# Hybrid decoder layer on one core: latent attention by four heads, with the query and key weights stationary and the results written turned

## The chip, the core and the metric

The kernel runs on one core of one Trainium2 chip. The metric is the device time of one execution in microseconds (us); lower is better. All arithmetic is in float32. The large products are made from two halves of each operand in the format fp32r (a high part and the rest), as hi*hi + hi*lo + lo*hi.

## The reference, cut to what matters

```python
SEQ = 256; N_HEADS = 16; Q_LORA_RANK = KV_LORA_RANK = 512
QK_NOPE_DIM = 128; QK_ROPE_DIM = 64; V_HEAD_DIM = 128
...
q = (rmsnorm(q_lat, g_q_a) @ w_q_b).reshape(B, S, N_HEADS, QK_NOPE_DIM + QK_ROPE_DIM)
q_nope, q_pe = q[..., :QK_NOPE_DIM], q[..., QK_NOPE_DIM:]
kv = (rmsnorm(c_kv, g_kv_a) @ w_kv_b).reshape(B, S, N_HEADS, QK_NOPE_DIM + V_HEAD_DIM)
k_nope, v = kv[..., :QK_NOPE_DIM], kv[..., QK_NOPE_DIM:]
...
q_pe = apply_rope(q_pe, cos, sin); k_pe = apply_rope(k_pe, cos, sin)
s = (einsum('bhqd,bhkd->bhqk', qn, kn) + einsum('bhqr,bkr->bhqk', qp, k_pe)) * scale
s = where(key_idx[None, :] <= q_idx[:, None], s, -inf)
o = einsum('bhqk,bhkd->bhqd', softmax(s), vh)
...
y_a = o @ w_attn_br
merged = sigmoid(gate_a) * y_a + sigmoid(gate_p) * y_p
```

`q_lat`, `c_kv`, `gate_a` and `gate_p` are columns of `rmsnorm(x) @ w_in`. The rest of the layer (pooling branch, memory cross-attention, feed-forward part) is the same in both kernels.

## The kernel before

All weights stream from memory in units. A unit is 2 contraction tiles of 128 rows times up to 512 columns. Two units make a chunk, which SyncE loads into one of four slots of `raw` (L403). For each unit ScalarE writes the high half `whi` (L1126, called hi below), VectorE the low half `wlo` (L1608, called lo), and TensorE multiplies (L571). There are four slots of `whi` and `wlo`: at step k ScalarE and VectorE prepare unit k + 4, and hi(k + 4) waits until TensorE is through with unit k (semaphore `w_used`). All orders are written out by hand; each engine waits on counting semaphores.

The attention loop has 4 turns (L728 on TensorE, L1264 on ScalarE, L1746 on VectorE, L449 on SyncE) of 2 pairs of heads. A pair has 12 units: units 0 and 1 make the queries of two heads (2 x 192 = 384 columns), units 2 and 3 keys and values of two heads (512 columns), units 4 to 11 a column of 512 of a gate. In all of them the activations (`lat` or `actA`, 128 tokens) are stationary and the weights move: for each contraction tile and each half t of the 256 tokens three matmuls (L566 to L568). The results land token by token in the two banks `acc`; half t = 0 of a unit is done before half t = 1, and ScalarE copies each half out (`evac`, L1140), which frees it for TensorE (`acc_out[t]`). Since the scores need queries and keys with the feature on the partitions, TensorE turns them:

```python
if k in (5, 6):            # head h = k - 5
    ...
    for t in range(TT):
        pe.transpose(at[(fs + h) % 2][:, t * P:(t + 1) * P],
                     q_sb[:, t, h * (NOPE + ROPE):h * (NOPE + ROPE) + NOPE], ident[:, :])
        mm = pe.transpose(at[(fs + h) % 2][:, S + t * P:S + (t + 1) * P],
                          kv_sb[:, t, 2 * h * P:(2 * h + 1) * P], ident[:, :])
```

After unit 6 two more transposes turn the rotated columns `qpe`, which VectorE made (`rotate`, L1662). Scores stand after units 7 and 8 (L764, L765), the transposes of the probabilities after unit 10 (L772), and the product with the values after unit 11 (L781, L783), that is behind the last unit of the gate. The gate of the first pair goes through a sigmoid into `bufX`, that of the second into `gp_sb`; GpSimd then multiplies `bufY` with `gp_sb` (L534). After the loop TensorE goes on with `w_attn_br` (`V_YA`), in the same two banks `acc`.

Ahead of the loop, ScalarE copies the latents to `zlat` and squares them, and TensorE turns the raw `zlat` into `lat`; the norm of each token (`rstd` of `N_Q` and `N_C`, L1635) is applied only at the copy out of queries, keys and values. The feed-forward input, further on, already has the other form that the change brings here: the weights stationary, both halves of the activations moving (512 columns, L979), and a second matmul of 256 columns with the low weights (L981). ScalarE copies one half of its result out (L1507), VectorE adds the other (L1978).

Of the kernel before, what the change touches and what calls it, by code (L numbers as in the profile page):

```python
# [35 lines left out]
AHEAD = 4  # L36
WARM_UP = 12
# [6 lines left out]
def hybrid_layer(nc, a, out, x3_spill):  # L44
# [15 lines left out]
    QPAIR = 2 * (NOPE + ROPE)  # L60
# [11 lines left out]
    V_YA = V_ATT + NH // 2 * 12  # L72
# [32 lines left out]
    U_YA = U_ATT + 3 * NH // 2  # L105
# [17 lines left out]
    A_MK = A_PAIR + 5 * NH // 2  # L123
# [13 lines left out]
    w_in, w_qb, w_kvb = rows("w_in"), rows("w_q_b"), rows("w_kv_b")  # L137
# [12 lines left out]
    def sem(name):  # L150
# [52 lines left out]
    q_sb = sb(pairs, "q_sb", [P, TT, QPAIR])  # L203
    kv_sb = sb(pairs, "kv_sb", [P, TT, NC])
    qkT = sb(pairs, "qkT", [P, 2, 2 * S])
    qpeT = sb(pairs, "qpeT", [P, S])
    qpe = sb(pairs, "qpe", [P, TT, 2 * ROPE])
# [55 lines left out]
    rdiag = cu[:, 1, :].rearrange("p (t s) -> p t s", t=TT)  # L263
    mq_sb = kch[:, :, :]
# [27 lines left out]
        "rope_step", "trig_ok", "abs_ok", "rope_ok", "ang_ok"))  # L292
    s_filled, s_max, s_nmax, s_exp, s_rsum, s_norm = (sem(n) for n in (
# [108 lines left out]
    def _(sp):  # L402
        def load(c, cs, src, n, kts=4):  # L403
# [4 lines left out]
            if n == NC:  # L408
                dst = raw[:, s, :, :].rearrange("p u (k n) -> p (u k) n", n=n)[:, 0:kts, :]
                sp.dma_start(dst, src).then_inc(w_loaded[s], 32)  # L410
            else:
                per = kts // 2
                for h in range(2):
                    dst = raw[:, s, h, 0:per * n].rearrange("p (k n) -> p k n", n=n)
                    sp.dma_start(dst, src[:, h * per:(h + 1) * per, :]).then_inc(w_loaded[s], 16)
# [33 lines left out]
        with sp.Fori(0, NH // 4) as i:  # L449
            for m in range(2):  # L450
                c = V_ATT // 2 + 12 * i + 6 * m
                load(c, 6 * m, w_qb[:, :, bass.ds(i * 2 * QPAIR + m * QPAIR, QPAIR)], QPAIR)
                load(c + 1, 6 * m + 1, w_kvb[:, :, bass.ds(i * 2 * NC + m * NC, NC)], NC)
                for j in range(4):
                    load(c + 2 + j, 6 * m + 2 + j,
                         w_in[:, 4 * j:4 * j + 4, bass.ds(i * NC + (C_GA, C_GP)[m], NC)], NC)
# [37 lines left out]
    def _(pool):  # L494
# [39 lines left out]
        with pool.Fori(0, ND) as i:  # L534
            for t in range(TT):
                pool.wait_ge(acc_out[t], U_ATT + 6 * i + 6)
# [19 lines left out]
    def _(pe):  # L556
# [71 lines left out]
        for v in range(16):  # L628
# [11 lines left out]
            if v in (10, 12):  # L640
                pe.wait_ge(acc_out[0], U_LAT + 1)
                pe.wait_ge(acc_out[1], U_LAT + 1)
# [85 lines left out]
        with pe.Fori(0, NH // 4) as i:  # L728
            for m in range(2):
                v, u, f = V_ATT + 24 * i + 12 * m, U_ATT + 6 * i + 3 * m, A_PAIR + 10 * i + 5 * m  # L730
                pair, fs = 2 * i + m, A_PAIR + 5 * m
                for k in range(12):
                    if k < 2:
                        unit(v + k, k, lambda h, kt: lat[:, h, kt, :], (2 * k, 2 * k + 1), QPAIR, u, k == 0, k == 1)
                    elif k < 4:
                        unit(v + k, k, lambda h, kt: lat[:, h, KL + kt, :], (2 * k - 4, 2 * k - 3), NC, u + 1,
                             k == 2, k == 3)
                    else:
                        unit(v + k, k, lhsA, (2 * k - 8, 2 * k - 7), NC, u + 2, k == 4, k == 11)
                    if k in (5, 6):  # L740
                        h = k - 5
                        for t in range(TT):
                            pe.wait_ge(acc_out[t], u + 2)
                        at_wait(f + h)
                        if k == 6:
                            pe.wait_ge(rope_ok, pair + 2)
                            at_wait(f + 2)
# [1476 lines left out]
```

## Time and profile before

| | us |
|---|---|
| median of 3 runs | 1797.07 (1796.44 to 1797.71) |
| the profiled execution: its own time | 1795.94 |
| its span in the trace | 1794.2 |
| TensorE busy | 1780.8 (99% of the span) |
| VectorE busy | 1155.4 (64%) |
| ScalarE busy | 951.6 (53%) |
| TensorE's granted clock | 0.999 of full |

The attention loop stands from about 164.8 to 469 us of the span. Matmuls overlap in the trace: what one costs is the distance between the starts of neighbours, not its duration. Where the next block has another shape, the cost of a short group is the start of the second matmul behind it, less where that would have stood without the group.

### The profile page before, as it was taken

The numbers are of one execution on the slowest core, as the hardware profiler recorded it, in microseconds if no ns is written. First come the engines' busy times: TensorE is split into PE (matmuls) and PEld (weight loads), VectorE is DVE, ScalarE is ACT, GpSimd is POOL, SyncE is SP. The second block draws the span as 40 slices with busy tenths as digits, with TensorE's granted clock in tenths as the row PEclk, the third lists the DMA queues.
The fourth block names the chain that finished last, engine by engine and source line by source line (L and its number), as shares of the span: only waits on it lengthen the run. The fifth ranks groups of instructions, "written<-read, shape, count | busy, mean of one in ns | idle before, by whom it ended". The sixth has DMA issues, their size and how long they took to land.

```text
span 1794.2 us, 25047 instructions
## 1 busy us (share of the span) xinstructions
PE 1780.8 (99%) x8758; PEld 1491.4 (83%) x8758; DVE 1155.4 (64%) x1608; ACT 951.6 (53%) x1295; POOL 59.4 (3%) x128
## 2 busy tenths in 40 slices
PE   9999999999999999999999999999999999999998
PEld 7888888888888888888888878888888888888786
DVE  5554555555465554454555477777777777788887
ACT  7555556665545655544555474444444444455554
POOL 4000000000000110000000100000000000000002
PEclk9999999999999999999999999999999999999999
DMA  8455544455466555555444546555555555656565
GB/s 287 153 188 176 166 162 148 156 170 168 167 222 221 201 189 176 183 173 190 154 146 158 189 166 232 187 187 187 187 187 187 187 187 187 199 167 206 190 197 189
DMA packets 167021, 330.74 MB, mean 184 GB/s; under 512 B 8454, under 2 KB 14006, under 8 KB 165558
## 3 DMA queue, kind: packets, MB, share of 16 engines
q1 hardware_dynamic: 165414, 318.48, 53.3%
q10 hardware_dynamic: 1552, 11.54, 1.6%
q8 instruction: 33, 0.54, 0.1%
q14 instruction: 22, 0.18, 0.0%
HBM read 325.81 MB, written 4.19 MB: 184 GB/s over the span
## 4 chain that ended last, share of the span: by engine, by line
PE 97%; DVE 1%; ACT 1%; DMA 0%; issue 0%; DVEq 0%; ACTq 0%
PE bank L566 17%; PE bank L979 17%; PE bank L568 17%; PE bank L567 17%; PE bank L981 9%; PE bank L1027 4%; PE bank L1028 4%; PE bank L1029 4%; PE bank L598 1%; PE bank L764 1%; PE bank L765 1%; PE bank L781 0%; PE bank L772 0%; DVE wlo L1605 0%; DVE actA L1926 0%; DMA bufX<-in_x 0%
## 5 line engine op out<-in xcount | busy, mean ns | idle before, releaser
L1605 DVE TENSOR_TENSOR wlo<-raw,whi 128x1024 fp32r<-128x1024 f32 x520 | 641.7, 1236 | 556.0 <-ACT whi L1138 433.0
L1138 ACT ACTIVATE whi<-raw 128x1024 fp32r<-128x1024 f32 x400 | 424.0, 1060 | 502.7 <-PE bank L568 293.0
L979 PE MATMUL bank<-actA,whi 128*128 128x512 f32 x1344 | 472.0, 394 | 0.0
L981 PE MATMUL bank<-actA,wlo 128*128 128x256 f32 x1344 | 380.1, 283 | 0.0
L979 PEld LDWEIGHTS bank<-actA,whi 128*128 128x128 f32 x1344 | 252.4, 188 | 58.3
L566 PE MATMUL bank<-whi,actA 128*128 128x512 f32 x672 | 273.2, 406 | 1.6 <-DVE wlo L1605 0.6
L568 PE MATMUL bank<-whi,actA 128*128 128x512 f32 x672 | 265.3, 395 | 0.0
L567 PE MATMUL bank<-wlo,actA 128*128 128x512 f32 x672 | 265.0, 394 | 0.0
L981 PEld LDWEIGHTS bank<-actA,wlo 128*128 128x128 f32 x1344 | 252.7, 188 | 0.0
L566 PE MATMUL bank<-whi,actB 128*128 128x512 f32 x576 | 229.2, 398 | 0.3 <-DVE actB L1620 0.3
L568 PE MATMUL bank<-whi,actB 128*128 128x512 f32 x576 | 227.3, 395 | 0.0
L567 PE MATMUL bank<-wlo,actB 128*128 128x512 f32 x576 | 227.2, 395 | 0.0
L1124 ACT ACTIVATE whi<-raw 128x1024 fp32r<-128x1024 f32 (+1 forms) x120 | 125.0, 1047 | 105.0 <-PE bank L568 90.7
L1543 ACT ACTIVATE whi<-raw 128x1024 fp32r<-128x1024 f32 x105 | 111.2, 1062 | 101.7 <-PE bank L1029 84.0
L566 PEld LDWEIGHTS bank<-whi,actA 128*128 128x128 f32 x672 | 126.6, 188 | 30.6 <-DVE wlo L1605 2.0
L568 PEld LDWEIGHTS bank<-whi,actA 128*128 128x128 f32 x672 | 126.4, 188 | 29.7
L2053 DVE TENSOR_TENSOR wlo<-raw,whi 128x1024 fp32r<-128x1024 f32 x105 | 129.2, 1232 | 31.5 <-ACT whi L1543 31.0
L567 PEld LDWEIGHTS bank<-wlo,actA 128*128 128x128 f32 x672 | 126.8, 189 | 26.6
L568 PEld LDWEIGHTS bank<-whi,actB 128*128 128x128 f32 x576 | 108.5, 188 | 25.5
L566 PEld LDWEIGHTS bank<-whi,actB 128*128 128x128 f32 x576 | 108.5, 188 | 24.6 <-DVE actB L1620 0.5
L567 PEld LDWEIGHTS bank<-wlo,actB 128*128 128x128 f32 x576 | 108.6, 188 | 24.3
L1027 PE MATMUL bank<-whi,gT 128*128 128x512 f32 x282 | 111.3, 395 | 0.4 <-DVE y L2131 0.4
(278 smaller groups left out, 1869.5 us busy)
## 6 DMA issues: line engine op xcount, KB each, us to landing
raw<-in_w_ffn_in SPq DMA_DIRECT2D x88, 1024.0 KB
raw<-in_w_in SPq DMA_DIRECT2D x48, 1024.0 KB
raw<-in_w_ffn_out SPq DMA_DIRECT2D x84, 512.0 KB, 4.9
raw<-in_w_mem_kv SPq DMA_DIRECT2D x32, 1024.0 KB
raw<-in_w_attn_br SPq DMA_DIRECT2D x16, 1024.0 KB
raw<-in_w_mix_out SPq DMA_DIRECT2D x16, 1024.0 KB
raw<-in_w_mem_q SPq DMA_DIRECT2D x16, 1024.0 KB
raw<-in_w_mem_o SPq DMA_DIRECT2D x16, 1024.0 KB
```

The source lines that it names most:

```text
L566: pe.matmul(acc[t][:, 0:n], hi, wh, start=f, stop=False)
L567: pe.matmul(acc[t][:, 0:n], hi, wl, start=False, stop=False)
L568: mm = pe.matmul(acc[t][:, 0:n], lo, wh, start=False, stop=l)
L979: pe.matmul(dst[:, :], whi[:, s, o:o + P], actA[:, :, kt, :], start=(kt == 0), stop=False)
L981: mm = pe.matmul(dst[:, 0:S], wlo[:, s, o:o + P], actA[:, 0, kt, :], start=False, stop=(kt == KD - 1))
L1027: pe.matmul(dst, hi, wh, start=first, stop=False)
L1028: pe.matmul(dst, hi, wl, start=False, stop=False)
L1124: act.activation(whi[:, vs % AHEAD, 0:w], raw[:, c, vs % 2, 0:w], ACT.Copy).then_inc(hi_done, 1)
L1138: act.activation(whi[:, ks % AHEAD, 0:w], raw[:, c, ks % 2, 0:w], ACT.Copy).then_inc(hi_done, 1)
L1543: act.activation(whi[:, n % AHEAD, :], form_at(u), ACT.Copy).then_inc(hi_done, 1)
L1605: dve.tensor_tensor(wlo[:, vs % AHEAD, 0:w], raw[:, c, vs % 2, 0:w], f32(whi[:, vs % AHEAD, 0:w]), ALU.subtract).then_inc(lo_done, 1)
L2053: dve.tensor_tensor(wlo[:, n % AHEAD, :], form_at(FOUT[n]), f32(whi[:, n % AHEAD, :]), ALU.subtract).then_inc(lo_done, 1)
```

## The change

The loop keeps 4 turns of 24 units, now for four heads at once: units 0 and 1 queries without the rotated columns, 2 and 3 rotated columns of four heads (256 columns), 4 and 5 keys, 6 and 7 values, 8 to 15 the gate of the pooled branch (`gp_sb`), 16 to 23 the gate of the attention branch (`bufX`). For queries and keys (`heads_unit`) the weights are stationary and the latents move, so that the results come out turned, in four banks, 2 to 5. Queries and keys use the same four banks one after the other. ScalarE copies the first 256 columns of each bank out (`heads_out`) and VectorE adds the others, behind its lo of the same step. The 16 transposes of a turn for queries and keys go. The two pairs of a turn (`pair_job`) then run behind units 6 to 12 and 14 to 20. Since keys and queries are turned, a token's norm can't be applied at the copy out any more: VectorE scales `zlat` itself (`latent_norm`), and TensorE's transposes of `zlat` wait for it (`z_ok`). A chunk of queries, rotated columns, keys or values is loaded by four DMAs with runs of 128 or 64 floats (`head_load`).

```diff
-    w_in, w_qb, w_kvb = rows("w_in"), rows("w_q_b"), rows("w_kv_b")
+    w_qb = a["w_q_b"][0].rearrange("(k p) (h n) -> p k h n", p=P, n=NOPE + ROPE)
+    w_kvb = a["w_kv_b"][0].rearrange("(k p) (h n) -> p k h n", p=P, n=NOPE + VD)
...
+        def head_load(c, cs, src, n):
+            s = cs % RAW_SLOTS
+            sp.wait_ge(lo_done, 2 * c - 2 * RAW_SLOTS + 2)
+            for k in range(4):
+                dst = raw[:, s, k // 2, k % 2 * QUAD * n:(k % 2 + 1) * QUAD * n].rearrange("p (h n) -> p h n", n=n)
+                sp.dma_start(dst, src[:, k, :, :]).then_inc(w_loaded[s], CHUNK_IN // 4)
...
@@ TensorE
             if v in (2, 4):
-                pe.wait_ge(acc_out[0], U_LAT + 2)
-                pe.wait_ge(acc_out[1], U_LAT + 2)
+                pe.wait_ge(z_ok, 4)
                 t_fill(T_C + (v - 2) // 2, (v - 2) // 2, zlat[:, 1, :, :], v - 2)
...
+        def heads_unit(v, vs, part_, k, first_filled):
+            s = vs % AHEAD
+            pe.wait_ge(lo_done, v + 1)
+            for b in range(2):
+                for kk in range(2):
+                    for j in range(2):
+                        o = kk * NC + (2 * b + j) * P
+                        kt = part_ + 2 * k + kk
+                        to = bank[2 + 2 * b + j]
+                        pe.matmul(to[:, :], whi[:, s, o:o + P], lat[:, :, kt, :], start=(k == 0 and kk == 0), stop=False)
+                        mm = pe.matmul(to[:, 0:S], wlo[:, s, o:o + P], lat[:, 0, kt, :],
+                                       start=False, stop=(k == 1 and kk == 1))
+                if b == 0 and k == 1:
+                    mm.then_inc(first_filled, 1)
+            mm.then_inc(w_used, 1)
...
+        with pe.Fori(0, NQ) as i:
+            v, u = V_ATT + 24 * i, U_ATT + 4 * i
+            for k in range(24):
+                if k < 2:
+                    if k == 0:
+                        pe.wait_ge(t_out, T_O + 2 * i)
+                    heads_unit(v + k, k, 0, k, q_filled)
+                elif k < 4:
+                    unit(v + k, k, lambda h, kt: lat[:, h, kt, :], (2 * k - 4, 2 * k - 3), QROPE, u, k == 2, k == 3)
+                elif k < 6:
+                    if k == 4:
+                        pe.wait_ge(q_sum, 2 * i + 2)
+                    heads_unit(v + k, k, KL, k - 4, k_filled)
+                elif k < 8:
+                    unit(v + k, k, lambda h, kt: lat[:, h, KL + kt, :], (2 * k - 12, 2 * k - 11), NC, u + 1,
+                         k == 6, k == 7)
+                else:
+                    c = k % 8
+                    unit(v + k, k, lhsA, (2 * c, 2 * c + 1), NC, u + 1 + k // 8, c == 0, c == 7)
+                for m in range(2):
+                    pair_job(i, m, k - 8 - 8 * m)
...
@@ ScalarE
+                if k == 1:
+                    heads_out(q_filled, i + 1, v + 2, [qT[:, 2 * b:2 * b + 2, :] for b in range(2)], q_copied_out)
...
+                if k == 15:
+                    act.wait_ge(k_sum, 2 * i + 2)
+                    evac(u + 2, v + 15, [gp_sb[:, t, :] for t in range(TT)], N_X, func=ACT.Sigmoid)
+                if k == 23:
+                    evac(u + 3, v + 23, [bufX[:, t, bass.ds(i * NC, NC)] for t in range(TT)], N_X, func=ACT.Sigmoid)
+                hi_at(V_ATT, i, 24, k)
...
@@ VectorE
+        def latent_norm(n, j):
+            dve.wait_ge(rstd_done, normed(n))
+            for t in range(TT):
+                dve.tensor_scalar(zlat[:, j, t, :], zlat[:, j, t, :], rstd[:, n, t:t + 1], None,
+                                  ALU.mult).then_inc(z_ok, 1)
...
+            for k in range(24):
+                lo_at(V_ATT, i, 24, k)
+                if k == 1:
+                    for b in range(2):
+                        dve.wait_ge(q_copied_out, 2 * i + b + 1)
+                        q = qT[:, 2 * b:2 * b + 2, :]
+                        dve.tensor_tensor(q, q, psum[:, 2 + 2 * b:4 + 2 * b, S:2 * S], ALU.add).then_inc(q_sum, 1)
```

**Between the queries and what uses the banks next.** On TensorE, after the change, these rows stand where the rotated columns (moving weights, 256 columns) end and the first key unit begins (stationary `whi`, moving `lat`).

```order
L588 MATMUL bank<-whi,lat 128x256
L586 MATMUL bank<-whi,lat 128x256
L587 MATMUL bank<-wlo,lat 128x256
L588 MATMUL bank<-whi,lat 128x256
L814 REGISTER_ALU
L749 REGISTER_ALU [waits q_sum]
L756 MATMUL bank<-lat,whi 128x512 [waits lo_done]
L757 MATMUL bank<-lat,wlo 128x256
```

The first key unit waits for `q_sum`, which VectorE gives after these rows, the first of a turn (lo of units 4 and 5, then the two additions). Before, the place of the additions was empty and no unit of the loop waited for VectorE to add.

```order
L1657 TENSOR_TENSOR wlo<-raw,whi 128x1024 [waits hi_done]
L1652 REGISTER_ALU
L1657 TENSOR_TENSOR wlo<-raw,whi 128x1024 [waits hi_done]
L1847 ISA
L1849 TENSOR_TENSOR qT<-qT,bank 128x512 [waits q_copied_out]
L1847 REGISTER_ALU
L1849 TENSOR_TENSOR qT<-qT,bank 128x512 [waits q_copied_out]
```

**Between the two gates.** On TensorE, before the change, the last unit of a pair's gate is followed by the product with the values, and then by the next unit in the banks `acc`:

```order
L568 MATMUL bank<-whi,actA 128x512
L776 REGISTER_ALU
L587 REGISTER_ALU [waits at_out]
L781 MATMUL bank<-probT,kv_sb 128x256 [waits t_out]
L783 MATMUL bank<-probT,kv_sb 128x128
L781 MATMUL bank<-probT,kv_sb 128x256
L783 MATMUL bank<-probT,kv_sb 128x128
L573 REGISTER_ALU
L561 REGISTER_ALU [waits lo_done]
L566 MATMUL bank<-whi,lat 128x384 [waits acc0_out]
L567 MATMUL bank<-wlo,lat 128x384
```

After it, the last unit of the first gate (unit 15) is followed at once by the first of the second gate (unit 16), which waits for bank 0 of `acc`:

```order
L586 MATMUL bank<-whi,actA 128x512
L587 MATMUL bank<-wlo,actA 128x512
L588 MATMUL bank<-whi,actA 128x512
L593 REGISTER_ALU
L581 REGISTER_ALU [waits lo_done]
L586 MATMUL bank<-whi,actA 128x512 [waits acc0_out]
L587 MATMUL bank<-wlo,actA 128x512
```

What moved: the four matmuls with `probT` stand behind units 12 and 20 now, and nothing stands between units 15 and 16. The same holds between unit 23 of the last turn and the first unit of `w_attn_br`.

**The copy out of a gate on ScalarE.** Before, the first pair's gate goes to `bufX`; the wait is an instruction of its own ahead of the load of the function table. After, the first gate of a turn goes to `gp_sb`, and the wait stands on the activation, behind the load (in the kernel before, the second pair's gate, to `gp_sb`, stands so too).

```order
L1185 ACTIVATE probT<-bank 128x384 [waits at_filled]
L1146 REGISTER_ALU [waits rstd_done]
L1150 ISA [waits acc0_ready]
L1150 ACT_TABLE_LOAD
L1150 ACTIVATE bufX<-bank,rstd 128x512
```

```order
L1176 ACTIVATE whi<-raw 128x1024 [waits w_used]
L1222 REGISTER_ALU
L1223 ACTIVATE qpeT<-bank 128x256 [waits at_filled]
L1342 REGISTER_ALU
L1184 REGISTER_ALU [waits rstd_done,k_sum]
L1188 ACT_TABLE_LOAD
L1188 ACTIVATE gp_sb<-bank,rstd 128x512 [waits acc0_ready]
```

## Rows read from the trace of the kernel before

**Rows 1.** The page, part 4: the chain that ended last.

```profile
PE 97%; DVE 1%; ACT 1%; DMA 0%; issue 0%; DVEq 0%; ACTq 0%
```

**Rows 2.** Waits of TensorE's weight loads, 170 to 440 us.

```profile
PEld bank L772 <- DVE prob L1768: 1.3, 7, 0.2
```

**Rows 3.** Timeline of TensorE: four transposes after a unit.

```profile
256.79 0.27 PE L749 MATMUL bank<-ident,q_sb 128*128 128x128 f32 x1
...
257.46 0.39 PE L567 MATMUL bank<-wlo,actA 128*128 128x512 f32 x1
```

**Rows 4.** Timeline of TensorE: 23 matmuls of 384 columns between these starts.

```profile
241.59 0.34 PE L567 MATMUL bank<-wlo,lat 128*128 128x384 f32 x1
...
245.63 0.39 PE L566 MATMUL bank<-whi,lat 128*128 128x512 f32 x1
```

**Rows 5.** Timeline of TensorE: 24 matmuls of 256 columns between these starts.

```profile
899.00 0.28 PE L885 MATMUL bank<-kvh,mqr 128*128 128x256 f32 x1
...
901.87 0.39 PE L566 MATMUL bank<-whi,actA 128*128 128x512 f32 x1
```

**Rows 6.** Timeline of TensorE: 17 pairs of 512 and 256 columns between.

```profile
1199.85 0.39 PE L979 MATMUL bank<-actA,whi 128*128 128x512 f32 x1
...
1205.81 0.40 PE L979 MATMUL bank<-actA,whi 128*128 128x512 f32 x1
```

**Rows 7.** Timeline of TensorE: the second half of a gate's last unit.

```profile
276.67 0.40 PE L566 MATMUL bank<-whi,actA 128*128 128x512 f32 x1
...
278.06 0.60 PE L781 MATMUL bank<-probT,kv_sb 128*128 128x256 f32 x2
```

**Rows 8.** Timeline of ScalarE: queries copied out, last unit done.

```profile
245.83 0.58 ACT L1150 ACTIVATE q_sb<-bank,rstd 128x384 f32<-128x384 f32 x1 [0.40 <-PE bank L568]
```

**Rows 9.** Timeline of ScalarE in the feed-forward part.

```profile
1212.77 1.09 ACT L1507 ACTIVATE asum<-bank 128x512 f32<-128x512 f32 x2 [1.31 <-PE bank L981]
1213.74 1.06 ACT L1138 ACTIVATE whi<-raw 128x1024 fp32r<-128x1024 f32 x1
```

**Rows 10.** Timeline of VectorE in the feed-forward part.

```profile
1214.83 1.22 DVE L1605 TENSOR_TENSOR wlo<-raw,whi 128x1024 fp32r<-128x1024 f32 x1 [2.43 <-ACT whi L1138]
1215.97 0.68 DVE L1998 TENSOR_TENSOR gT<-cu,gT 128x512 f32 x1
1216.58 1.23 DVE L1605 TENSOR_TENSOR wlo<-raw,whi 128x1024 fp32r<-128x1024 f32 x1
```

**Rows 11.** Timeline of ScalarE: first copy out of the loop.

```profile
169.02 1.03 ACT L1150 ACTIVATE q_sb<-bank,rstd 128x384 f32<-128x384 f32 x2
```

**Rows 12.** Timeline of TensorE: it waits for that copy.

```profile
168.91 0.34 PE L568 MATMUL bank<-whi,lat 128*128 128x384 f32 x1
169.63 0.51 PE L566 MATMUL bank<-whi,lat 128*128 128x512 f32 x1 [0.38 <-ACT q_sb L1150]
169.98 0.39 PE L567 MATMUL bank<-wlo,lat 128*128 128x512 f32 x1
```

**Rows 13.** Timeline of ScalarE: the two gates, and a copy of 256 columns.

```profile
238.53 1.28 ACT L1150 ACT_TABLE_LOAD   x1
239.82 1.26 ACT L1150 ACTIVATE gp_sb<-bank,rstd 128x512 f32<-128x512 f32 x2
...
276.96 1.28 ACT L1150 ACT_TABLE_LOAD   x1 [0.50 <-PE bank L568]
...
299.62 0.38 ACT L1185 ACTIVATE qpeT<-bank 128x256 f32<-128x256 f32 x1
```

**Rows 14.** Groups of VectorE by line and form: busy us, mean ns, idle before.

```profile
L1768 DVE TENSOR_SCALAR prob<-prob,rsum 128x256 f32<-128x256 f32 x16 | 5.6, 348 | 0.0
```

**Rows 15.** Timeline of VectorE: the norm of the key latents.

```profile
66.77 0.17 DVE L1635 RECIPROCAL rstd<-std 128x2 f32<-128x2 f32 x1 [0.27 <-ACT std L1161]
```

**Rows 16.** Timeline of TensorE: the transposes of the key latents.

```profile
67.45 0.60 PE L598 MATMUL bank<-ident,zlat 128*128 128x128 f32 x4
```

**Rows 17.** Stretch of 2 us: engines, clock, DMA share, GB/s (columns of 64).

```profile
80.00:82.00 2.00, 2.00 (x10) 1.64 (x9) 1.14 (x1) 1.52 (x2) 0.00 (x0) 1.00 0.58 131
```

More of the change, by code:

```diff
@@ L59, in hybrid_layer @@
     NF = DFF // NC
[L60 removed]
+    QUAD = 4
+    NQ = NH // QUAD
+    QROPE = QUAD * ROPE
     SCALE = float((NOPE + ROPE) ** -0.5)
@@ L202, in hybrid_layer @@
     pairs = ExitStack()
-    q_sb = sb(pairs, "q_sb", [P, TT, QPAIR])
-    kv_sb = sb(pairs, "kv_sb", [P, TT, NC])
-    qkT = sb(pairs, "qkT", [P, 2, 2 * S])
+    qr_sb = sb(pairs, "qr_sb", [P, TT, QROPE])
+    v_sb = sb(pairs, "v_sb", [P, TT, NC])
+    qT = sb(pairs, "qT", [P, QUAD, S])
     qpeT = sb(pairs, "qpeT", [P, S])
-    qpe = sb(pairs, "qpe", [P, TT, 2 * ROPE])
+    qpe = sb(pairs, "qpe", [P, 2, TT, 2 * ROPE])
     prob = sb(pairs, "prob", [P, 2, 3 * P])
@@ L263, in hybrid_layer @@
     rdiag = cu[:, 1, :].rearrange("p (t s) -> p t s", t=TT)
+    k_half = [gp_sb[:, b, :].rearrange("p (h s) -> p h s", h=2) for b in range(TT)]
     mq_sb = kch[:, :, :]
@@ new lines, in normalise, with pair_job @@
+        def normalise(n, h):
+            dve.wait_ge(s_exp, 2 * n + 2)
+            dve.reciprocal(rsum[:, h, :], ssum[:, h, :]).then_inc(s_rsum, 1)
+            dve.wait_ge(s_rsum, n + 1)
+            for t in range(TT):
+                o = slice(t * P, (2 * t + 1) * P)
+                dve.tensor_scalar(prob[:, h, o], prob[:, h, o], rsum[:, h, t:t + 1], None,
+                                  ALU.mult).then_inc(s_norm, 1)
+        def pair_job(i, m, k):
+            pair = 2 * i + m
+            if k == 0:
+                row_max(2 * pair, 0)
+            if k == 1:
+                row_max(2 * pair + 1, 1)
+                normalise(2 * pair, 0)
+            if k == 2:
+                normalise(2 * pair + 1, 1)
+            if k == 4:
+                t_split(T_O + pair, T_O + m, *tiles(actB, 4 * i + 2 * m))
@@ new lines, in _ @@
+        with dve.Fori(0, NQ) as i:
+            for k in range(24):
+                lo_at(V_ATT, i, 24, k)
+                if k == 1:
+                    for b in range(2):
+                        dve.wait_ge(q_copied_out, 2 * i + b + 1)
+                        q = qT[:, 2 * b:2 * b + 2, :]
+                        dve.tensor_tensor(q, q, psum[:, 2 + 2 * b:4 + 2 * b, S:2 * S], ALU.add).then_inc(q_sum, 1)
+                if k == 5:
+                    for b in range(2):
+                        dve.wait_ge(k_copied_out, 2 * i + b + 1)
+                        dve.tensor_tensor(bufX[:, b, bass.ds(i * NC, NC)].rearrange("p (h s) -> p h s", h=2), k_half[b],
+                                          psum[:, 2 + 2 * b:4 + 2 * b, S:2 * S], ALU.add).then_inc(k_sum, 1)
+                if k in (3, 4):
+                    m, pair = k - 3, 2 * i + k - 3
+                    if m == 0:
+                        for t in range(TT):
+                            dve.wait_ge(acc_out[t], U_ATT + 4 * i + 1)
+                    rotate([qr_sb[:, :, (2 * m + h) * ROPE:(2 * m + h + 1) * ROPE] for h in range(2)],
+                           [qpe[:, m, :, h * ROPE:(h + 1) * ROPE] for h in range(2)], steps[0] + pair, pair + 1)
+                for m in range(2):
+                    pair_job(i, m, k - 8 - 8 * m)
```

249 lines of the change are left out of this document (105 added, 144 removed).

## The prediction

> **What bounds the kernel now.** I read the page first, and there the chain that ended last: 97% of it is TensorE [rows 1]. The reader is to see that a microsecond of TensorE work saved or a microsecond of waiting added on TensorE moves the end, and that nothing else does. Then the waits of TensorE's weight loads over the attention loop: in 270 us the only entry is the wait for the normalised probabilities, 7 times, 1.3 us in all [rows 2]. So ScalarE and VectorE stay ahead of TensorE throughout the loop, with little to spare where a chain of theirs is long. Last I read the timelines of the three engines, row by row, over one turn of the loop and over the feed-forward part, which already has the form that is brought in here.
>
> **What TensorE no longer does, and what it does in another form.** Four transposes start at 256.79; the second matmul behind them starts at 257.46, where it would have stood at 256.79 + 0.23 = 257.02. So four cost 0.44 us, 0.11 each [rows 3]. 16 a turn, 64 in all go: **-7.0 us**. The multiplications keep their columns (43008 a turn) but are cut otherwise. Prices from starts: 384 columns (245.63 - 241.59)/23 = 0.1757 us [rows 4]; 512 columns (278.06 - 276.67)/6 = 0.232 [rows 7]; 256 columns (901.87 - 899.00)/24 = 0.1196 [rows 5]; a pair of 512 and 256 with stationary weights (1205.81 - 1199.85)/17 = 0.3506 [rows 6]. A turn before: 48 x 0.1757 + 48 x 0.232 = 19.57. After: 32 x 0.3506 + 24 x 0.1196 + 24 x 0.232 = 19.66. Four turns: **+0.3 us**. The row for 256 columns is of stationary activations and moving fp32r, as the rotated columns are; were they bound by the weight load instead, a turn's 24 would take more, but the wait of the next paragraph would shrink by the same amount.
>
> **The wait for the query sums.** Keys go into the banks in which the queries still lie, and between the two stand only the two short units of rotated columns, 24 x 0.1196 = 2.87 us. Count from S, the start of the first of these units. ScalarE sees unit 1 done 0.20 later (245.83 against 245.63) [rows 4, 8]. It copies the second half of the queries out and then makes hi of unit 5: in the feed-forward part the second of two such copies takes (1213.74 - 1212.77)/2 = 0.49, so hi starts at S + 0.69 [rows 9]. VectorE's lo starts 1.09 behind hi (1214.83 against 1213.74), at S + 1.78; the next operation starts 1.14 later, at S + 2.92; one of 512 columns takes 0.68 and its neighbour starts after 0.61 [rows 9, 10]. So the two additions end at S + 2.92 + 0.61 + 0.68 = S + 4.21. From a release to where TensorE effectively goes on it takes 0.15: the first copy of the loop starts at 169.02 and its first half is out 0.58 later, at 169.60, and the matmul after the next starts at 169.98, that is 0.23 behind an effective start of 169.75 [rows 8, 11, 12]. The key unit starts at S + 4.36 instead of S + 2.87: 1.5 us a turn, **+6.0 us**. Queued behind it are all of TensorE's later units; what is late next on ScalarE (hi of unit 8, which waits for unit 4) has four units of lead, and its lo comes 6 us ahead of need. The key sums lie in the open: between them and their first reader stand units 6 to 8.
>
> **The wait between the two gates.** Before, the product with the values stood behind each gate's last unit, and the copy out with its sigmoid lay under it; no wait for it is in the trace [rows 2]. After, unit 16 follows unit 15 and needs bank 0. Count from U, where unit 15's predecessor ends and the two transposes of `qpe` start: unit 16 would start at U + 0.22 + 2.78 = U + 3.00. ScalarE starts hi of unit 18 at U + 0.20, is free for the copy of `qpe` about 1.0 later and through with it at U + 1.6 [rows 13]. The load of the table then isn't held by unit 15 (238.53 follows the copies without a gap) and the sigmoid starts 1.29 behind it; two copies out take 1.26, the first some 0.67 [rows 13]. Bank 0 is free at U + 1.6 + 1.29 + 0.67 = U + 3.55, TensorE goes on at U + 3.70: 0.7 a turn, **+2.7 us**.
>
> **At the loop's end** the first unit of `w_attn_br` follows unit 23 directly. That gate goes to `bufX`, and there the load is held by the first half: it starts 0.29 after the second half's first matmul (276.96 against 276.67) [rows 7, 13]. Bank 0 is free 0.29 + 1.29 + 0.67 = 2.25 after that point, TensorE goes on at 2.40 instead of 1.39: **+1.0 us**, once. Between turns there is no such wait, since unit 0 writes to other banks and unit 2 comes 5.6 us later.
>
> **At the loop's start** the queries before waited for their own predecessor's copy: 169.75 against a start of 168.91 + 0.18 = 169.09. The two query units now use no bank that ScalarE still has to read: **-0.7 us** [rows 12].
>
> **The norm of the latents.** The reciprocal starts at 66.77 and takes 0.17; two scalings of 512 columns follow. The nearest row is such a scaling of 256 columns, 0.35 [rows 14, 15]. Below: two of that row overlap, and there is next to no wait. Above: at the rate of an operation with two tensors, 66.97 + 0.61 + 0.68 = 68.26, TensorE's transposes going on at 68.41 instead of 67.45 [rows 10, 16]: 1.0 us. I take 0.47 for one and 0.38 to the next, done at 67.8: **+0.5 us**. The query latents have more room, two whole units, and cost nothing; the cover there is the two units between their squares and their transposes, and without it they would cost the whole chain, some 2 us.
>
> **At nothing:** the copies out of queries and keys (ScalarE has four copies fewer of turned tiles), the other place of the pairs (scores, exponentials and transposes keep their distances in units, so the waits of [rows 2] stay), GpSimd's product in mid-turn (it lies beside lo of unit 19, which has two units of lead), and the loads.
>
> **The sum:** -7.0 + 0.3 + 6.0 + 2.7 + 1.0 - 0.7 + 0.5 = +2.8, with the digits kept +2.9. On the profiled execution's 1795.94 (its span is 1794.2) that is 1798.8; the median of the runs shown is 1.1 higher, so I predict 1797.07 + 2.9 = **1800.0 us**. 0.2%, which is about what a measurement can tell here, is 3.6 us: faster is below 1793.5, slower above 1800.7.
>
> **The loads and a rule against them.** A 2 us stretch with two loads in runs of 256 bytes shows 131 GB/s at a busy share of 0.58, so 226 GB/s at full share [rows 17]. A chunk of 1 MB at that rate takes 4.6 us, and each has about six units, some 16 us, from its issue to its use. Cost nothing; bounds: nothing, and the rival below.
>
> The Trainium skill ("DMA: Bandwidth & Descriptors", Specifications) wants at least 512 bytes for line rate, and below that has a read-modify-write; the rotated columns come in 256 bytes. By the rule that chunk is slow in a way that it gives no figure for; the row above bears out a lower rate, and the rival takes it up.
>
> **Rivals.**
> *Slower, by the table load (0.20).* If unit 15 holds the load of the table, as with `bufX` [rows 13], each turn's wait is 2.25 + 0.15 - 1.39 = 1.0 instead of 0.7. For it: an exponential's table stands in between in both cases, and the row that speaks against it has other copies ahead. Price 4 x 0.33 = 1.3: 1801.3, slower. It decides from 0.2 us a turn on.
> *Slower, by a longer change of table (0.02).* Five copies out on TensorE's path carry a load. If a change took twice the 1.29 of [rows 13], each would end 1.29 later: +6.5, 1806.5. Against it: in both rows the sigmoid, or what ScalarE does next, starts when the load is over.
> The Trainium skill ("ScalarE: Activation LUTs", What ACT_TABLE_LOAD costs) has such a rule: it adds a drain of 1380 ns to the 1283 ns of the load, which would make the sum, as an estimate, 1807. The trace agrees with the 1283, and shows no drain: 1.29 from the load's start to the sigmoid's.
> *Slower, by late loads (0.06).* Four chunks a turn come in four pieces each, 16 issues of SyncE in a row. If their data came at a third of the rate above, a 1 MB chunk would take 14 us, four 56, and the eight units that use them last 20, with 16 of lead: some 20 us a turn. At half the rate they take 37, and the wait is about 1 us a turn: 1804. Against it: the share of 0.58 for small runs.
> *Faster (0.07).* The sums are ready in time: if VectorE's additions came ahead of TensorE, the 6.0 would go: 1794.0, and with half of the gate's wait gone too 1792.6. Against it: the additions stand behind lo of unit 5 in the order, and lo can't start before hi. It needs three of the steps in my chain to be shorter by a third.
> *Half of the wait (0.10).* The chain from S is shorter by 0.7 us, because the copy or lo starts sooner: 1797.1, no change.
> *The forecast (0.55)*, own range 1798.4 to 1801.6 by 0.3 either way in each of five waits; a quarter of it is above 1800.7.
>
> **The numbers.** Faster 0.07. Slower 0.20 + 0.02 + 0.06 + a quarter of 0.55 = 0.42. Same: three quarters of 0.55 + 0.10 = 0.51. The range 1796 to 1803 holds the forecast, the half wait and the held load, 0.85, and leaves out the others.
>
> **What would show it.** After: no transposes of queries and keys; the weight loads of the first key matmul wait for VectorE's addition 4 times, some 1.5 us each; those of the second gate's first unit wait for the copy to `gp_sb` 4 times, 0.7 each, and of `w_attn_br` once for `bufX`, 1.0; one wait of 0.5 for `zlat`; the query wait at 169 gone; rotated columns at 0.12 a matmul; no wait of hi for a load. I am wrong if another wait appears in the loop, if the key wait is under 1 us, or if hi waits for data.

## The result, and the profile after

| | before | after |
|---|---|---|
| median | 1796.82 us (20 runs, 1795.89 to 1797.71) | 1799.61 us (20 runs, 1798.71 to 1800.32) |
| span of the profiled execution | 1794.2 us | 1797.6 us |

The ratio is 1.0015, with a 95% interval of 1.0009 to 1.0021: the changed kernel is 2.8 us slower. Forecast were +2.9 and 1800.0 us. By the border that the prediction sets itself (slower above 1800.7) this counts as no change; the interval nevertheless excludes 1.

The page of the changed kernel, its first lines and part 4 (the chain that ended last):

```profile
span 1797.6 us, 25146 instructions
PE 1776.7 (99%) x8758; PEld 1483.8 (83%) x8758; DVE 1165.5 (65%) x1628; ACT 941.2 (52%) x1279; POOL 60.7 (3%) x128
PE 95%; DVE 2%; ACT 1%; issue 1%; DMA 0%; DVEq 0%; ACTq 0%
```

TensorE is busy for 4 us less than before and the span is longer: it has less to do and waits more. The chain of [rows 1] has fallen from 97% to 95% TensorE; 1% more is VectorE's, and 1% is "issue" (TensorE or another engine waiting for nothing that the profile shows).

The waits of TensorE's matmuls over the whole of the changed kernel (us in total, times, longest) say for what:

```profile
PE bank L756 <- DVE qT L1849: 5.3, 4, 1.3
PE bank L586 <- ACT gp_sb L1188: 1.7, 4, 0.4
...
PE bank L586 <- ACT bufX L1188: 0.8, 1, 0.8
...
PE bank L618 <- DVE zlat L1693: 0.3, 1, 0.3
```

None of these four was there before, and each is one that the prediction names. The waits of the weight loads in the attention loop, against [rows 2]:

```profile
PEld bank L756 <- issue: 6.1, 4, 1.5
PEld bank L586 <- ACT gp_sb L1188: 3.4, 4, 0.9
PEld bank L788 <- DVE prob L1826: 1.5, 8, 0.2
PEld bank L586 <- issue: 1.2, 1, 1.2
```

The wait for the probabilities is as it was (1.5 us in 8 waits, 1.3 in 7 before). The wait for the copy at the start of the loop [rows 12] has gone.

**The key unit's wait.** Timeline of turn 2 (start, duration, engine, line); rows of TensorE between the first and the last of the rotated columns' matmuls are left out:

```profile
247.27 0.28 PE L586 MATMUL bank<-whi,lat 128*128 128x256 f32 x1
...
247.47 0.60 ACT L1309 ACTIVATE qT<-bank 128x512 f32<-128x512 f32 x1 [0.57 <-PE bank L757]
...
247.96 2.00 ACT L1176 ACTIVATE whi<-raw 128x1024 fp32r<-128x1024 f32 x2
...
249.04 1.23 DVE L1657 TENSOR_TENSOR wlo<-raw,whi 128x1024 fp32r<-128x1024 f32 x1 [1.36 <-ACT whi L1176]
...
250.00 0.28 PE L588 MATMUL bank<-whi,lat 128*128 128x256 f32 x1
...
250.19 1.28 DVE L1849 TENSOR_TENSOR qT<-qT,bank 128x512 f32<-128x512 f32 x2
...
251.60 0.49 PE L756 MATMUL bank<-lat,whi 128*128 128x512 f32 x1 [1.31 <-DVE qT L1849]
...
251.93 0.27 PE L757 MATMUL bank<-lat,wlo 128*128 128x256 f32 x1
```

Read it down: copy of the queries, hi of unit 5 (at S + 0.69, S being 247.27), lo of unit 5, the two additions, and only then keys. TensorE was through with the rotated columns at 247.27 + 24 x 0.119 = 250.13 and goes on effectively at 251.93 - 0.23 = 251.70: 1.57 us, forecast 1.5. The other three turns show the same 1.57.

**The wait between the gates.** ScalarE in turn 1, then TensorE:

```profile
212.47 1.28 ACT L1188 ACT_TABLE_LOAD   x1
213.77 1.27 ACT L1188 ACTIVATE gp_sb<-bank,rstd 128x512 f32<-128x512 f32 x2
```
```profile
213.69 0.39 PE L588 MATMUL bank<-whi,actA 128*128 128x512 f32 x1
214.51 0.51 PE L586 MATMUL bank<-whi,actA 128*128 128x512 f32 x1 [0.42 <-ACT gp_sb L1188]
214.85 0.39 PE L587 MATMUL bank<-wlo,actA 128*128 128x512 f32 x1
```

The table load is not held by the gate's last unit; the sigmoid starts 1.30 behind it. The matmul after the next stands at 214.85, where an unbroken stream has it at 213.69 + 2 x 0.232 = 214.15: 0.7 us, and 0.67 to 0.70 in the other turns. At the loop's end the load is held by the unit, as forecast, and the same reckoning gives 472.29 - (470.74 + 0.46) = 1.09 us (ScalarE, then TensorE):

```profile
469.85 1.28 ACT L1188 ACT_TABLE_LOAD   x1 [0.41 <-PE bank L588]
```
```profile
470.74 0.40 PE L588 MATMUL bank<-whi,actA 128*128 128x512 f32 x1
471.98 0.47 PE L586 MATMUL bank<-whi,actB 128*128 128x512 f32 x1 [0.84 <-ACT bufX L1188]
472.29 0.39 PE L587 MATMUL bank<-wlo,actB 128*128 128x512 f32 x1
```

The key latents' transposes are late too: the second matmul behind them starts at 68.64 instead of 68.12, 0.5 us. The Trainium skill ("ScalarE: Activation LUTs", What ACT_TABLE_LOAD costs) has 1283 ns for the load, and the trace agrees (1.28 us). The drain of 1380 ns that the same section adds is in no row here: the sigmoid starts 1.30 us behind the start of the load.

### The profile page after: what moved, and what is told of

It is laid out like the page before. It is cut to its first block, busy times and chain, and to the rows that moved or that the text cites. A ratio compares the mean times of both kernels' runs of the same rounds, so it can differ in the third digit from the quotient of the medians.

```text
span 1797.6 us, 25146 instructions
## 1 busy us (share of the span) xinstructions
PE 1776.7 (99%) x8758; PEld 1483.8 (83%) x8758; DVE 1165.5 (65%) x1628; ACT 941.2 (52%) x1279; POOL 60.7 (3%) x128
## 2 busy tenths in 40 slices
DMA packets 192237, 330.75 MB, mean 184 GB/s; under 512 B 17286, under 2 KB 43318, under 8 KB 190774
## 4 chain that ended last, share of the span: by engine, by line
PE 95%; DVE 2%; ACT 1%; issue 1%; DMA 0%; DVEq 0%; ACTq 0%
PE bank L1017 17%; PE bank L586 16%; PE bank L588 16%; PE bank L587 16%; PE bank L1019 9%; PE bank L1065 4%; PE bank L1066 4%; PE bank L1067 4%; PE bank L756 2%; PE bank L618 1%; PE bank L757 1%; PE bank L779 1%; PE bank L781 1%; PE bank L797 0%; PE bank L788 0%
```

## The experiments

The third column is the kernel before on the same chip. "Span" is that of the profiled execution. The runs stand on several chips, on which the kernel before took between 1796.11 and 1796.90 us, so a difference of medians between two rows can be off by some tenths; the spans are given beside it where it matters.

| run | median | before | span |
|---|---|---|---|
| additions first | 1793.31 | 1796.90 | 1791.6 |
| gates split | 1793.32 | 1796.90 | 1792.0 |
| both | 1787.21 | 1796.90 | 1785.8 |
| before, 48 transposes less | 1791.13 | 1796.90 | 1788.7 |
| additions later | 1808.39 | 1796.11 | 1807.0 |
| plain loads | 1799.47 | 1796.11 | 1797.2 |
| both, key latents later | 1786.61 | 1796.11 | 1784.9 |
| 32 bytes | 1796.78 | 1796.45 | 1795.0 |
| both, no tile | 1789.56 | 1796.45 | 1787.7 |
| 64 bytes | 1788.21 | 1796.45 | 1786.4 |
| 32 bytes ahead of the weights, 32 behind | 1796.84 | 1796.45 | 1795.0 |
| all, 64 bytes | 1777.86 | 1796.75 | 1775.3 |

### The wait for the query sums

```diff
-                lo_at(V_ATT, i, 24, k)
                 if k == 1:
                     for b in range(2):
                         dve.wait_ge(q_copied_out, 2 * i + b + 1)
                         ...
                         dve.tensor_tensor(q, q, psum[...], ALU.add).then_inc(q_sum, 1)
+                lo_at(V_ATT, i, 24, k)
```

> The changed kernel with VectorE's two additions of the query sums put ahead of the subtraction of unit 5, and nothing else moved. In the changed kernel the key transposes of every turn wait for these sums: the second addition ends when the clock row of the trace has it at 251.5 in turn 2, and TensorE stands still for 251.93 - 0.23 - 250.13 = 1.57 us there, 6.28 us over four turns. My theory: with the additions first they end one subtraction (1.2 us and its wait for the rounded weights) sooner, the wait goes, and the kernel takes about 6.2 us less than the changed one, some 3.4 us less than the kernel before: 1793.4 us. Rival one: the wait is set by the sums of TensorE or by ScalarE's copy and not by the order on VectorE; then nothing changes (1799.6). Rival two: the subtraction that now comes later holds unit 5's low weights back by about as much as was won; then the wait moves to the first product of unit 5 and the time is between 1797 and 1799.6.

Measured 1793.31, ratio to before 0.9978 (0.9969 to 0.9987), so 6.3 us under the changed kernel, where 6.2 were expected. VectorE in turn 2 of this kernel:

```profile
246.04 1.28 DVE L1848 TENSOR_TENSOR qT<-qT,bank 128x512 f32<-128x512 f32 x2
247.49 2.36 DVE L1657 TENSOR_TENSOR wlo<-raw,whi 128x1024 fp32r<-128x1024 f32 x2 [0.17 <-ACT whi L1176]
```

The additions fill the time in which VectorE waited for hi, the subtraction behind them is on time, and no wait for `qT` is left. The term of +6.0 is shown, and both rivals fall. The other direction, `if k == 2` in place of `if k == 1` and nothing else:

> The changed kernel with VectorE's two additions of the query sums put one unit later, behind the subtraction of unit 6 rather than of unit 5. The same cause as for additions first, with the other sign. Theory: the key transposes now wait for the additions behind one subtraction more, some 1.1 us a turn by the rows of turn 2 (subtraction of 1.2 us, of which the engine's idle time takes a little off), 4.6 us in all: 1804.2 us. Rival: the wait is set elsewhere and has slack towards VectorE, then 1799.6.

Measured 1808.39: slower, as it should be, but by 8.8 us and not 4.6. The waits give what they were to give:

```profile
PE bank L756 <- DVE qT L1849: 9.8, 4, 2.5
```

9.8 - 5.3 = 4.5 us. Most of the rest is the clock. Stretches of 1 us in turn 2 (columns: stretch, its length, PE busy with its count, granted clock, DMA share, GB/s) and one in turn 3, and the first matmul behind the loop:

```profile
254.00:255.00 1.00, 0.00 (x0) 1.00 0.69 88
255.00:256.00 1.00, 0.59 (x1) 0.55 0.95 336
...
257.00:258.00 1.00, 1.00 (x5) 0.50 1.15 244
258.00:259.00 1.00, 1.00 (x6) 0.74 0.58 90
259.00:260.00 1.00, 1.00 (x8) 1.00 1.01 393
...
335.00:336.00 1.00, 1.00 (x8) 1.00 1.05 408
```
```profile
481.03 0.47 PE L586 MATMUL bank<-whi,actB 128*128 128x512 f32 x1 [0.84 <-ACT bufX L1188]
```

TensorE idles 2.45 us and the granted clock then stands at 0.50, that is 1.2 GHz, for over 3 us. In 10 us from 250 the mean is 0.83, and the same 0.83 stands in turns 1 and 4; in turn 3, after a wait as long, the clock stays at 1.00, and no run shows why. What it costs is read from the starts: the first matmul behind the loop comes 481.03 - 471.98 = 9.05 us later than in the changed kernel, 4.5 of it the waits, so 1.5 for each of the three turns. The spans differ by 9.4 us (medians on two chips: 8.8); the remaining 0.3 comes behind the loop. The five runs bear the clock out: the one with a mean clock of 0.998 took 1806.01, the four at 0.995 or 0.996 took 1808.25 to 1811.18. In the changed kernel the clock over these waits, 1.57 us long, is 1.00 throughout.

### The gates

```diff
-                    evac(u + 2, v + 15, [gp_sb[:, t, :] for t in range(TT)], N_X, func=ACT.Sigmoid)
+                    evac(u + 2, v + 15, [gp_sb[:, t, :] for t in range(TT)], N_X)
...
+                if k == 21:
+                    for t in range(TT):
+                        act.wait_ge(acc_out[t], u + 3)
+                    act.activation(gp_sb[:, :, :], gp_sb[:, :, :], ACT.Sigmoid).then_inc(gp_sig, 1)
```

The same for `bufX` at step 23. There a small copy into a new tile `tick` of one element a partition stands ahead of the sigmoid; GpSimd and the merge wait for `gp_sig` and `ga_sig`.

> The changed kernel with the gates taken out of their banks by a plain copy (as the projections of the queries are), so that the bank is free without a change of function table, and the sigmoid done later on the copy in its own memory, behind the rounding of later weights. The results are the same. In the changed kernel the unit behind the first gate's waits 0.69 us a turn for the gate's bank (2.76 us over four turns), and the unit behind the last gate 1.09 us once. My theory: both waits go, 2.8 + 1.1 = 3.9 us, so 1795.7 us. Rival: the waits between the gates are not set by the table load but by the length of the activation itself (1.26 us a pair), then at most half of it goes, 1797.6 us or more. Second rival: the later sigmoids delay ScalarE's rounding of weights and give it back as waits of TensorE for high weights; then 1799.6 or more.

Measured 1793.32: 6.3 us gone, where 3.9 were expected. ScalarE in turn 1 of this kernel:

```profile
213.64 0.69 ACT L1190 ACTIVATE gp_sb<-bank,rstd 128x512 f32<-128x512 f32 x1 [0.30 <-PE bank L590]
215.04 0.69 ACT L1190 ACTIVATE gp_sb<-bank,rstd 128x512 f32<-128x512 f32 x1 [0.72 <-PE bank L590]
...
237.67 1.28 ACT L1352 ACT_TABLE_LOAD   x1
238.96 1.06 ACT L1352 ACTIVATE gp_sb<-gp_sb 128x1024 f32<-128x1024 f32 x1
```

The bank is read at once, and load and sigmoid lie where nobody waits; the waits for `gp_sb` and `bufX` are gone from the list. So the mechanism is right, and 2.4 us too many need another cause. They are in no wait: TensorE's feed-forward stage, which the edit doesn't touch, is shorter (460.34 us instead of 466.24), and stages that move weights are a little longer. Next, both edits:

> The two edits of the runs before together: additions first, and gates copied out before their sigmoid. The waits stand at different places of a turn, so my theory adds them: 1799.6 - 6.2 - 3.9 = 1789.5 us, 7.3 us less than the kernel before. That is also the kernel before's -7.0 us of transposes at 0.11 us each with the new waits taken away. Rival: transposes left out give less than 0.11 us each and the sum of the new waits is smaller than the trace's records say; then it lies between 1791 and 1795.

1787.21: again 2.3 under expectation, while the two edits add up (6.3 + 6.3 = 12.6, measured 12.4). The same with the small copy going to the existing tile `warm`, so that no tile is added:

> Additions first and gates split as in both edits together, with the small copy that carries the wait going into a tile that is there already, so that no tile is added and all addresses are those of the changed kernel. Theory: the waits alone are taken away here: 1799.6 - 6.3 (additions first, measured) - 3.9 (gates by the trace) = 1789.4 us, and the feed-forward part is back at 0.1756 us. Rival: the split of the gates gives its whole 6.3 us by itself; then 1787.2 as with the tile.

1789.56, 0.2 beside the theory. From additions first, the gates are worth 1793.31 - 1789.56 = 3.75 us, where the terms +2.7 and +1.0 say 3.7. (The two stand on different chips: the spans differ by 3.9, the distances to the kernel before by 3.3.) The other 2.4 belonged to the tile.

### The address of the tiles

```diff
     warm = sb(ctx, "warm", [P, TT])
+    sb(ctx, "pad", [P, 8])
     part = sb(ctx, "part", [P, 9, TT, 4])
```

> The changed kernel with one unused tile of 32 bytes a partition ahead of the sums of squares, so that all tiles that come later (activations, latents, buffers) begin 32 bytes later in every partition, at 32 beyond a multiple of 64 instead of at a multiple of 64; no instruction is added. The gates' split saved 6.3 us where 3.9 were expected, and it brought a small tile at this place; in its trace the feed-forward part's 2656 products run at 0.1734 us each and not 0.1756 (5.9 us less), and the products of units that move 512 columns at 0.2334 and not 0.2324 (some 4 us more over the kernel). Theory: it is the address of the tiles; then this kernel shows both paces and takes 1.8 to 2.4 us less than the changed kernel, 1797.4 us. Rival: the pace comes from the instructions that the split moved (the place of code or other work beside it); then it stays at 1799.6, with 0.1756.

> The changed kernel with an unused tile of 64 bytes at the same place, so that the later tiles move but lie at multiples of 64 bytes again. Theory (address within 64 bytes decides): nothing changes, 1799.6 us, feed-forward products at 0.1756. Rival: any move of the tiles does it (which of them share some larger block); then about 1797.4 as with 32 bytes, or another time altogether.

> The changed kernel with 32 bytes unused ahead of the rounded weights and 32 more ahead of the sums of squares: the weights' tiles lie at 32 beyond a multiple of 64, the activations at a multiple of 64 again. If the operand that moves is what decides, with 32 beyond as the faster place: the units, where weights move, run faster than 0.2324 and the feed-forward part, where activations move, stays at 0.1756. If it is the distance between moving and held operand: the feed-forward part goes to 0.1734 and the units to 0.2334, as with the 32 bytes behind the weights, 1797.4 us. If it is the held operand: the feed-forward part, which holds weights, changes, and the units stay at 0.2324.

Measured 1796.78, 1788.21 and 1796.84. First and last matmul of a stage of 288 matmuls that move 512 columns of weights, and of the feed-forward stage; the changed kernel first:

```profile
776.80 0.48 PE L586 MATMUL bank<-whi,actB 128*128 128x512 f32 x1
...
843.58 0.39 PE L588 MATMUL bank<-whi,actB 128*128 128x512 f32 x1
...
1086.12 0.48 PE L1017 MATMUL bank<-actA,whi 128*128 128x512 f32 x1
...
1552.36 0.29 PE L1019 MATMUL bank<-actA,wlo 128*128 128x256 f32 x1
```

With 32 bytes:

```profile
778.66 0.48 PE L587 MATMUL bank<-whi,actB 128*128 128x512 f32 x1
...
845.73 0.40 PE L589 MATMUL bank<-whi,actB 128*128 128x512 f32 x1
...
1088.91 0.48 PE L1018 MATMUL bank<-actA,whi 128*128 128x512 f32 x1
...
1549.26 0.28 PE L1020 MATMUL bank<-actA,wlo 128*128 128x256 f32 x1
```

With 64 bytes:

```profile
769.48 0.47 PE L587 MATMUL bank<-whi,actB 128*128 128x512 f32 x1
...
835.25 0.39 PE L589 MATMUL bank<-whi,actB 128*128 128x512 f32 x1
...
1075.90 0.48 PE L1018 MATMUL bank<-actA,whi 128*128 128x512 f32 x1
...
1545.09 0.28 PE L1020 MATMUL bank<-actA,wlo 128*128 128x256 f32 x1
```

| from `whi` to `actA` | weights move: 288 matmuls | feed-forward: 2656 matmuls |
|---|---|---|
| 35712 bytes (changed) | 66.78 us | 466.24 us |
| + 32 | 67.07 | 460.35 |
| + 32, `whi` itself moved by 32 | 67.06 | 460.34 |
| + 64 | 65.77 | 469.19 |

The 35712 bytes are counted from the tiles' declarations, each rounded up to 32; no run prints an address, but `tick`, of 4 bytes, gives the feed-forward stage the same 460.34 us as the pad of 32.

The second and third rows are the same to 0.01 us with the tiles at other addresses: it is the distance between the tile that moves and the tile that is held, not where either lies. Of the expectations, those by the address within 64 bytes fail at + 64, those by the distance hold at the one place that tells them apart. Over the whole kernel, up to the first matmul of the feed-forward stage, + 32 falls 2.8 us behind the changed kernel (1088.91 against 1086.12) and + 64 gets 10.2 ahead (1075.90). In the stage + 32 wins 5.9 and + 64 loses 3.0. Behind it, to the end of the spans, + 32 loses another 0.5 and + 64 wins 3.9. In all they are 2.6 and 11.2 us faster by the spans, 2.8 and 11.4 by the medians. What in the memory makes it so is open; three distances out of many were tried.

The stages that move weights need a caution. The next one, of 300 matmuls, in the changed kernel and in additions first, whose tiles lie at the same addresses:

```profile
978.36 0.50 PE L586 MATMUL bank<-whi,actB 128*128 128x512 f32 x1 [0.26 <-DVE actB L1672]
...
1047.94 0.40 PE L588 MATMUL bank<-whi,actB 128*128 128x512 f32 x1
```
```profile
971.98 0.50 PE L586 MATMUL bank<-whi,actB 128*128 128x512 f32 x1 [0.26 <-DVE actB L1672]
...
1041.84 0.40 PE L588 MATMUL bank<-whi,actB 128*128 128x512 f32 x1
```

These are 69.58 and 69.86 us; with 32 bytes it is 69.87, with 64 bytes 68.56. Both edits without a tile have the 69.86 too, and additions later has the slower pace in both stages. So the 0.3 us a stage that + 32 loses also occurs with no tile moved, and that it comes from the distance is not shown. The 1.0 us that + 64 wins in each stage is beyond that. The feed-forward stage has no such scatter: 466.22 to 466.24 us in all seven kernels with the tiles unmoved, 460.34 in all five with + 32 (`tick` or a pad), 469.18 and 469.19 in the two with + 64.

The kernel before and the changed one have `whi`, `wlo`, `actA`, `actB` and `lat` at the same addresses, and their feed-forward stages take 466.22 and 466.24 us, the two stages that move weights 66.78 and 69.58 in both. The comparison of the two is free of this effect.

### The transposes, the loads, and what was left

```diff
-                        for t in range(TT):
-                            pe.transpose(at[(fs + h) % 2][:, t * P:(t + 1) * P], q_sb[...], ident[:, :])
-                            mm = pe.transpose(at[(fs + h) % 2][:, S + t * P:S + (t + 1) * P], kv_sb[...], ident[:, :])
+                        mm = pe.transpose(at[(fs + h) % 2][:, S:S + P], kv_sb[:, 0, ...], ident[:, :])
```

> The kernel before with 48 of its 64 transposes of queries and keys left out: of each group of four into one bank only one remains, with the copies out of the bank and everything else as they were. It leaves part of the turning out, so its queries and keys are not the reference's. It measures the term of -7.0 us by itself: at 0.11 us each (the transposes lie in a stream of products that TensorE does not wait in) 48 cost 48 x 0.11 = 5.3 us, so 1791.5 us. Rival one: a transpose costs what its weight load and its product take by themselves, 0.3 us or more; then over 14 us would go, 1782 us. Rival two: they are hidden in waits of TensorE for other engines; then nothing changes (1796.8).

1791.13 against 1796.90: 5.8 us, 0.12 for each transpose. The traces give a little less. The first matmul of the feed-forward stage, in the kernel before and in this run:

```profile
1083.21 0.47 PE L979 MATMUL bank<-actA,whi 128*128 128x512 f32 x1
```
```profile
1077.70 0.47 PE L976 MATMUL bank<-actA,whi 128*128 128x512 f32 x1
```

That is 5.5 us, 0.115 for each. Both rivals fall; all 64 are worth 7.7 by the medians, 7.3 by these starts, 7.0 by the rows of the prediction.

The loads: in the changed kernel each group of four pieces became one load,

```diff
-            head_load(c, 0, w_qb[:, :, heads, 0:NOPE], NOPE)
+            one_load(c + 0, 0, w_in[:, 0:4, bass.ds(i * NC, NC)])
```

and the other three likewise.

> The changed kernel with the four chunks of a turn that gather columns of four heads (many short pieces) loaded as one contiguous chunk of the same size each. It leaves the real query, key and value weights of these units out, so its output isn't the reference's; all instructions and waits are the same, and the packets under 512 B of the loop are gone. Theory: the loads land long before they are needed and no rounding of weights in the loop waits for a transfer, so nothing changes: 1799.6 within 0.2%. Rival: short pieces load the queues that other transfers need, and some of the +2.8 us is theirs; then 1797 to 1798.5.

1799.47 against the changed kernel's 1799.61: the pieces cost nothing that can be measured, though the changed kernel has 17286 packets under 512 bytes and the kernel before 8454. One thing differs from the expectation's words: the chunk of rotated columns was half as large, so this run loads 2.1 MB more (332.84 instead of 330.75).

The key latents' transposes, `if v in (2, 4)` made `(3, 5)`, and the copies out with them:

> Additions first and gates copied out before their sigmoid, and besides the turning of the key latents, which fills time of TensorE behind units 2 and 4, put behind units 3 and 5. Theory: the key transposes come a unit later relative to the query sums' copies, so what is left of their wait after additions first (some 0.1 us a turn by my reckoning) goes too: about 0.5 us less than both edits alone, 1789.0 us. Rival: nothing is left to take away and it is equal to both edits alone; or the later turning delays units behind it and it is slower by 0.5 to 2 us.

This expectation names the wrong wait. The transposes that the edit moves lie ahead of the loop, and what can go there is their wait for the latents' norm. The list of waits shows it gone (0.3 before the edit), and the span is 0.9 shorter than with both edits, 0.5 of it where the edit is and 0.4 at the kernel's start, where nothing was changed; but on its chip the kernel before was 0.8 faster too, and the ratios, 0.9945 and 0.9947, are the same. The 0.5 us are seen in the trace and not told apart by the times.

Last, all of it, `tick` replaced by a pad of 64 bytes:

> Additions first, gates split without a tile of its own, key latents turned one unit later (where they no longer wait for their norm), and 64 unused bytes a partition ahead of the activations as in the run of 64 bytes. If the causes are apart the gains add: 1799.6 - 6.3 (additions) - 3.8 (gates, from both edits without a tile) - 0.6 (latents later) - 11.4 (64 bytes) = 1777.5 us, 19.3 us less than the kernel before. Rival: with TensorE's products closer together the other engines come late for more of them and part of the 11.4 us goes into new waits; then 1779 to 1785.

1777.86 (four runs), ratio 0.9898 (0.9882 to 0.9915): 18.9 us faster than the kernel before, 21.7 than the changed one. Expected were 1777.5. The gains add up, so the waits and the distance are separate causes.

## Why the prediction was right

| term | forecast | trace of the changed kernel | run |
|---|---|---|---|
| 64 transposes | -7.0 | | -7.3 (starts) to -7.7 (medians), from 48 left out |
| matmuls cut otherwise | +0.3 | +0.3 (pairs at 0.3506, rotated columns at 0.119) | |
| query sums | +6.0 | 4 x 1.57 = +6.3 | 6.3, additions first |
| between the gates | +2.7 | 4 x 0.69 = +2.8 | 3.75 with the next term |
| end of the loop | +1.0 | +1.1 | (both without a tile, against additions first) |
| start of the loop | -0.7 | the wait is gone | |
| norm of the latents | +0.5 | +0.5 | not told apart |
| sum | +2.9 | +3.2, with the forecast's -7.0 | |

With the -7.3 of the starts the terms make +2.9, with the -7.7 of the medians +2.5. The first matmul of the feed-forward stage starts at 1083.21 before and at 1086.12 after: 2.9 us later. The medians say 2.8, the spans 3.4; the other 0.5 of the spans comes behind that matmul, where the two kernels do the same, and the run with plain loads (span 1797.2) hasn't got it. Every wait came where the chains of the three engines put it, within 0.1 us.

*The rival of the held table load* is refuted by the row at 212.47: no idle time stands before it, while the one ahead of `bufX` at the loop's end is held for 0.41 us, as was forecast. *A longer change of table*: 1.30 from load to sigmoid, refuted. *Late loads*: no hi waits for data in the loop, and plain loads gave nothing. *Half of the wait*: 1.57, not half. *Faster*: it would have needed the additions ahead of TensorE; putting them there by hand gave the time that the rival named (1794.0, measured 1793.3).

Where the working was thin: the weight of one transpose came from a single gap of 0.44 us and is 5 to 10% small by the run, 0.3 to 0.7 us in all, while the wait for the query sums was 0.3 us larger than forecast. The two errors have opposite signs. That the sum came out within 0.1 us of the medians is partly luck; the mechanism, wait by wait, is not.

## What to carry to other kernels

Work taken off the bounding engine can come back as waits, if the new form brings a producer and its consumer closer together. Here some 7 us of transposes went, but the keys go into the banks that the queries have just filled (6.3 us), and two gates' units follow each other in the same bank (2.8 and 1.1). So walk every chain (copy out, rounding, addition) from its release to its first reader, and look for the engine whose next instruction waits for something else: moving the additions into that idle time, one line, was worth 6.3 us, and reading a bank with a plain copy and applying the function later another 3.8. And when an edit adds or resizes a tile, compare the length of a stage that it doesn't touch, before explaining the difference by the edit.

## What the runs showed of the hardware that was not expected

**Distance of the two operands.** TensorE's pace in an unbroken stream depends on how far apart moved and held tile lie. For the feed-forward mix of 512 and 256 columns a matmul takes 0.1756 us at 35712 bytes, 0.1734 at 32 more and 0.1767 at 64 more. A matmul of 512 columns of weights takes 0.2327 at 35712 bytes and 0.2292 at 64 more; the 0.2337 at 32 more also occurs at 35712 in three of the runs. Over this kernel 64 unused bytes are 11.4 us, four times the effect of the change under study. The Trainium skill ("TensorE: Matmul & The Clock Gate", Step-by-step: what each phase is for) says that moved operand and weight load have read ports of their own, so that a weight load takes no read bandwidth from the matmul that runs. These stages, in which nothing waits and only addresses differ, show a pace that hangs on where the two lie, by 0.6 to 1.5%, which that sentence doesn't foresee; whether it is the ports that meet is not shown.

**The clock after a wait.** Idle times of 1.6 us left the granted clock at 1.00 each time; after 2.45 us it stood at 0.50 (1.2 GHz) for some 3 us in three turns of four, and cost 1.5 us each time, more than the 1.1 us by which the wait had grown.
